# Expert layer: 128 of 512 tokens by gathered weight rows and VectorE sums, 384 by dense products, result with tokens on partitions

## The chip, the core and the metric

One core of a Trainium2 chip runs the whole kernel. Its engines run their own queues and meet only at semaphores: TensorE (PE, with its weight loads PEld), VectorE (DVE), ScalarE (ACT), GpSimd (POOL) and SyncE (SP), which only issues DMAs. The metric is the device time of one execution in microseconds.

## The reference, cut to what matters

Two blocks run one after the other on 512 tokens of width 1024: attention, pooling, convolution and a gated feed-forward, then three attentions, merged, and an expert layer. The change is in that last layer alone.

```
s1, s2 = q[..., 0, :] @ keys1.T, q[..., 1, :] @ keys2.T      # 8 heads, 128 keys each
v1, i1 = top_k(s1, 16);  v2, i2 = top_k(s2, 16)
sv, si = top_k(v1[..., :, None] + v2[..., None, :], 16)       # 16 of 256 pairs
experts = e1 * 128 + e2;  gates = softmax(sv)                 # 8 * 16 = 128 experts a token, of 16384
a   = einsum('cd,ced->ce', h, u[experts])                     # u, v: 16384 x 1024
act = gelu(a) * gates
out = einsum('ce,ced->cd', act, v[experts])
x   = x + out
```

## The kernel before

No row of `u` or `v` is looked up. All 16384 experts are computed for all 512 tokens, and a dense table of gates, zero nearly everywhere, selects. Weights come as slabs of 128 x 2048 (1 MB) in one stream; SyncE loads them into two `raw` buffers, GpSimd splits each into a high and a low part (`W_hi`, `W_lo`), and each exact product is three products (high x high, high x low, low x high), so that TensorE issues three matmuls, each with its weights loaded anew.

The expert layer runs over these stages:

- For each of 8 heads: the query product, scores (TensorE), the two top 16 and the top 16 of pairs (VectorE). One slab of `u` is multiplied beside each head (`u_half`, 2 x 8 x 3 matmuls of 512 tokens a slab), then 8 more slabs while VectorE turns the choices into expert numbers and gates (`picks`). ScalarE applies gelu to each result and stores it in HBM (`gelu_dram`).
- The other 48 slabs of `u`. For each token VectorE makes two one-hot rows (lines 1673 and 1674), and TensorE multiplies them (line 802) into the token's 128 x 128 table of gates; ScalarE collects 64 tokens and stores 4 MB (`gates_dram`). TensorE issues one such product after every three matmuls of `u_half`. 4 of 6 slabs have tokens beside them (16 each).
- 64 slabs of `v`. For each, SyncE loads the gelu values and the gates of its 256 experts (a pair, `gelu_in` and `g_in`), VectorE multiplies them (`gated`, line 1681), ScalarE copies the product to `B_hi` (line 1220), VectorE subtracts for `B_lo` (line 1687), and TensorE adds 48 matmuls into all eight banks, features on partitions (`outputs_of`, lines 817 to 819). At the end VectorE adds the banks to X, and one DMA stores 2 MB.

Every engine's order is the order in which the code is written; nothing is scheduled. GpSimd splits slab s (`split_whole`, lines 379 to 385) when it is loaded (`slab_loaded`) and TensorE has used slab s-2 (`slab_used`). Its `slab_split` releases TensorE and also SyncE's next load into that `raw` buffer. A pair is loaded when the pair two before has been multiplied (`act_ready`).

Of the kernel before, what the change touches and what calls it, by code (L numbers as in the profile page):

```python
# [35 lines left out]
GB = T // GT  # L36


U_PICKS, U_TOKENS, U_BETWEEN = 8, 4, 2
assert HEADS + U_PICKS + GB * (U_TOKENS + U_BETWEEN) == PAIRS and GT % (8 * U_TOKENS) == 0  # L40
U_AT = HEADS + U_PICKS

# [29 lines left out]
ARENA = 19170  # L72
# [14 lines left out]
def build(nc, x_in, stream, cols_in, tables_in, mem_in, keys_in, out):  # L87
    g_dram = nc.dram_tensor("gates_dram", [GB, P, KEYS, GT], F32, kind="Internal").ap()
    gelu_dram = nc.dram_tensor("gelu_dram", [PAIRS, P, 2 * T], F32, kind="Internal").ap()

    with ExitStack() as ctx:
# [21 lines left out]
        tab = sb("tab", [P, 512])  # L113
        col = sb("col", [P, N_COLS])
# [8 lines left out]
        bank = [ctx.enter_context(nc.psum_tensor(f"bank{i}", [P, 512], F32)) for i in range(8)]  # L123
# [54 lines left out]
        top_f = [bank[1 + q // 2][:, 256 * (q % 2):256 * (q % 2) + 256].rearrange("p (h s) -> p h s", h=HEADS)  # L178
# [4 lines left out]
        picks_t = at(16384, 3, T)  # L183
        iota = at(17920, KEYS)
        hot = at(18048, 4, 2, KEYS)
# [4 lines left out]
        gelu_in, g_in, prod = at(0, 2, 2 * T), at(2048, 2, 2 * T), at(4096, 2, 2 * T)  # L190
        gelu_out = B_plain[:, 0:4, :]

# [6 lines left out]
        slab_half = sem("slab_half")  # L199
# [33 lines left out]
        x_done, stored = sem("x_done"), sem("stored")  # L233

# [73 lines left out]
        def _(sp):  # L308
# [40 lines left out]
            def pair(s, j):  # L349
# [7 lines left out]
                sp.dma_start(gelu_in[:, j, :], gelu_dram[s + j, :, :]).then_inc(pair_loaded[j], 16)  # L357
# [12 lines left out]
            sp.wait_ge(x_done, 1)  # L370
            sp.dma_start(out.rearrange("(k p) t -> p k t", p=P), X[:, :, :]).then_inc(stored, 16)
            sp.wait_ge(stored, 16)
# [3 lines left out]
        def _(pool):  # L376
            def split_whole(s, j, ada=N_ADA - 4):

                pool.wait_ge(slab_loaded[j], s * 8 + (8 * ada + 16))
                pool.wait_ge(slab_used, s + (j - 1))  # L380
                pool.tensor_tensor(beat[:, :], zero[:, :], zero[:, :], ALU.add)  # L381
                pool.tensor_copy(W_hi[:, j, :], raw[:, j, :]).then_inc(slab_half, 1)  # L382
                pool.wait_ge(slab_half, s + (IN_PARTS * (PARTS - 1) + j + 1))
                pool.tensor_tensor(W_lo[:, j, :], raw[:, j, :], W_hi[:, j, :].bitcast(F32), ALU.subtract)\  # L384
                    .then_inc(slab_split, 1)
# [42 lines left out]
            if n % 2:  # L428
                split_whole(n - 1, 0)
# [3 lines left out]
        def _(pe):  # L433
# [309 lines left out]
            def u_half(s, odd, j, before=N_MID, token=None):  # L743
# [3 lines left out]
                if not isinstance(s, int) or s + odd > 0:  # L747
                    pe.wait_ge(gelu_ready, s * 2 + (2 * odd + j - 1))
                for k in range(KD):
                    (lh, ll), (rh, rl) = w_tile(slot, D * j + P * k), act_tile("A", k)  # L750
                    mm(bank[6 + j][:, :], lh, rh, start=k == 0, stop=False)  # L751
                    mm(bank[6 + j][:, :], lh, rl, start=False, stop=False)  # L752
                    last = mm(bank[6 + j][:, :], ll, rh, start=False, stop=k == KD - 1)  # L753
# [28 lines left out]
            for q in range(QT):  # L782
# [8 lines left out]
            for q in range(GB):  # L791
                per_half = GT // (2 * U_TOKENS)
                first = U_AT + (U_TOKENS + U_BETWEEN) * q
                with pe.Fori(0, U_TOKENS - 1, 2) as s:
                    t = s * (2 * per_half)
                    for half in range(4):
                        def token(k):
                            j = per_half * half + k
# [7 lines left out]
                u_slabs(first + U_TOKENS, U_BETWEEN)  # L806


            def outputs_of(s, odd, first=False, final=False):
# [3 lines left out]
                for j in range(2):  # L813
                    for m in range(KD):
                        lh, ll = w_tile(slot, D * j + P * m)
                        rh, rl = act_tile("B", 4 + 2 * odd + j)
                        mm(bank[m][:, :], lh, rh, start=first and j == 0, stop=False, skip_group_check=True)  # L817
                        mm(bank[m][:, :], lh, rl, start=False, stop=False, skip_group_check=True)  # L818
                        last = mm(bank[m][:, :], ll, rh, start=False, stop=final and j == 1, skip_group_check=True)  # L819
                last.then_inc(slab_used, 1)  # L820

            pe.wait_ge(g_copied, T + 8)
            pe.wait_ge(gelu_ready, KEYS)
            outputs_of(0, 0, first=True)
            outputs_of(0, 1)
            with pe.Fori(2, PAIRS - 3, 2) as s:
                for odd in range(2):
                    outputs_of(s, odd)
# [5 lines left out]
        def _(act):  # L834
# [310 lines left out]
            def gelus(s, odd=0, tokens=None):  # L1145
# [3 lines left out]
                for j in range(2):  # L1149
# [11 lines left out]
                    act.activation(out_[:, j, :], bank[6 + j][:, :], ACT.Gelu).then_inc(gelu_ready, 1)  # L1161
# [69 lines left out]
        def _(dve):  # L1231
# [459 lines left out]
            for j in range(2):  # L1691
                gated(0, j)
# [139 lines left out]
```

## Time and profile before

| | |
|---|---|
| median of 3 runs | 3113.04 us (3111.86 to 3113.2) |
| the profiled execution | 3113.2 us, its span 3111.4 us |
| busy | PE 94%, POOL 55%, DVE 49%, ACT 21% |
| granted TensorE clock, whole span | 0.967 |
| expert layer, from the first scores | 1458 to 3111 us |

A matmul's recorded duration (0.39 us for 512 columns) holds its latency in the pipeline; its cost in a stream is the distance between two starts. A DMA is recorded at its issue on its queue (SPq, ACTq), and the time to its landing stands in the DMA view. An idle time in brackets in a timeline is that just before the row, with what ended it.

### The profile page before, as it was taken

The page shows a single profiled execution, that of the slowest core. Times are in us where ns is not written, and L with a number is a line of the kernel's source. Part 1 is how long each engine was busy: PE and PEld are TensorE (multiplying, and loading weights), DVE is VectorE, ACT ScalarE, POOL GpSimd, SP SyncE. Part 2 cuts the span into 40 slices and gives each one's busy share as a digit, 9 for nine tenths or more (in the row PEclk, how much of TensorE's full clock was granted, in tenths as well). Part 3 has the DMA queues.
Part 4 walks back from the last instruction along what each step waited for, and adds up shares of the span by engine and source line. Part 5 has one row for each costly group of instructions (what it writes and reads, how often), then busy time and mean ns, then how long its engine had stood idle before and what let it go on. Part 6 is the DMA issues. An engine that isn't in the chain of part 4 may idle for free.

```text
span 3111.4 us, 40021 instructions
## 1 busy us (share of the span) xinstructions
PE 2915.2 (94%) x13606; PEld 2346.7 (75%) x13606; DVE 1528.7 (49%) x2999; ACT 659.0 (21%) x1262; POOL 1703.2 (55%) x1248
## 2 busy tenths in 40 slices
PE   4977799998999899998999999999998999999998
PEld 3855588886866656776877888888887888888886
DVE  4466421113432344544889555555554555555553
ACT  4167110002223243331001111121111010000000
POOL 3745466766511615664555445544454666666664
PEclk8988899999989999999999999999999999999999
DMA  5223222222100212212233344444446455555553
GB/s 229 95 90 138 78 82 95 95 95 99 68 28 28 71 41 70 94 68 89 108 110 122 118 173 176 162 176 169 176 167 218 168 196 196 195 189 189 190 196 127
DMA packets 126527, 402.18 MB, mean 129 GB/s; under 512 B 7504, under 2 KB 74704, under 8 KB 93904
## 3 DMA queue, kind: packets, MB, share of 16 engines
q1 hardware_dynamic: 113280, 328.75, 30.2%
q10 hardware_dynamic: 13136, 71.89, 5.9%
q8 instruction: 77, 1.26, 0.2%
q14 instruction: 34, 0.28, 0.0%
HBM read 331.40 MB, written 69.21 MB: 129 GB/s over the span
## 4 chain that ended last, share of the span: by engine, by line
PE 88%; DVE 5%; ACT 3%; DMA 1%; issue 1%; POOL 1%; ACTq 0%; SPq 0%; DVEq 0%; POOLq 0%
PE bank L487 8%; PE bank L489 8%; PE bank L488 8%; PE bank L817 7%; PE bank L819 7%; PE bank L818 7%; PE bank L751 7%; PE bank L752 7%; PE bank L753 7%; PE bank L802 4%; PE bank L617 2%; PE bank L635 2%; PE bank L593 2%; PE bank L637 1%; PE bank L636 1%; PE bank L521 1%
## 5 line engine op out<-in xcount | busy, mean ns | idle before, releaser
L384 POOL TENSOR_TENSOR W_lo<-raw,W_hi 128x2048 fp32r<-128x2048 f32 x127 | 637.9, 5023 | 10.2
L400 POOL TENSOR_TENSOR W_lo<-raw,W_hi 128x512 fp32r<-128x512 f32 x376 | 494.0, 1324 | 0.0
L751 PE MATMUL bank<-A_hi,W_hi 128*128 128x512 f32 x1024 | 449.2, 439 | 3.9 <-ACT B_plain L1161 2.9
L817 PE MATMUL bank<-B_hi,W_hi 128*128 128x512 f32 x1024 | 399.1, 390 | 10.3 <-DVE B_lo L1687 10.3
L752 PE MATMUL bank<-A_lo,W_hi 128*128 128x512 f32 x1024 | 403.5, 394 | 0.0
L753 PE MATMUL bank<-A_hi,W_lo 128*128 128x512 f32 x1024 | 403.5, 394 | 0.0
L819 PE MATMUL bank<-B_hi,W_lo 128*128 128x512 f32 x1024 | 398.8, 389 | 0.0
L818 PE MATMUL bank<-B_lo,W_hi 128*128 128x512 f32 x1024 | 398.8, 389 | 0.0
L403 POOL TENSOR_TENSOR beat<-zero 128x1 f32<-128x1 f32 x94 | 19.3, 205 | 658.1 <-PE bank L637 255.8
L381 POOL TENSOR_TENSOR beat<-zero 128x1 f32<-128x1 f32 x127 | 24.6, 194 | 638.6 <-PE bank L753 401.8
L1673 DVE TENSOR_SCALAR arena<-bank,arena 128x128 f32<-128x128 f32 x512 | 179.7, 351 | 301.8 <-PE bank L802 282.0
L1681 DVE TENSOR_TENSOR arena<-arena 128x1024 f32<-128x1024 f32 x64 | 232.3, 3630 | 141.5 <-DMA arena<-gates_dram 141.5
L487 PE MATMUL bank<-A_hi,W_hi 128*128 128x512 f32 x680 | 265.8, 391 | 4.9 <-issue 4.9
L489 PE MATMUL bank<-A_hi,W_lo 128*128 128x512 f32 x680 | 264.7, 389 | 0.0
L488 PE MATMUL bank<-A_lo,W_hi 128*128 128x512 f32 x680 | 264.6, 389 | 0.0
L395 POOL CAST W_hi<-raw 128x512 fp32r<-128x512 f32 x376 | 248.6, 676 | 0.0
L382 POOL CAST W_hi<-raw 128x2048 fp32r<-128x2048 f32 x127 | 241.1, 1899 | 0.0
L1687 DVE TENSOR_TENSOR B_lo<-arena,B_hi 128x1024 fp32r<-128x1024 f32 x64 | 132.2, 2066 | 208.4 <-ACT B_hi L1220 208.4
L817 PEld LDWEIGHTS bank<-B_hi,W_hi 128*128 128x128 f32 x1024 | 192.6, 188 | 50.6 <-issue 10.6
L802 PEld LDWEIGHTS bank<-arena 128*128 128x128 f32 x1024 | 193.0, 188 | 46.5
L753 PEld LDWEIGHTS bank<-A_hi,W_lo 128*128 128x128 f32 x1024 | 192.4, 188 | 45.3
L818 PEld LDWEIGHTS bank<-B_lo,W_hi 128*128 128x128 f32 x1024 | 192.6, 188 | 40.0
(234 smaller groups left out, 5207.3 us busy)
## 6 DMA issues: line engine op xcount, KB each, us to landing
raw<-weights SPq DMA_DIRECT2D x241, 1024.0 KB, 4.8
gelu_dram<-B_plain ACTq DMA_DIRECT2D x64, 512.0 KB, 2.6
gates_dram<-arena ACTq DMA_DIRECT2D x8, 4096.0 KB, 14.9
arena<-gelu_dram SPq DMA_DIRECT2D x64, 512.0 KB, 5.6
arena<-gates_dram SPq DMA_DIRECT2D x64, 512.0 KB, 6.9
W_plain<-weights SPq DMA_DIRECT2D x4, 1024.0 KB, 15.9
X<-x_t SPq DMA_DIRECT2D x1, 2048.0 KB, 14.1
out_t<-X SPq DMA_DIRECT2D x1, 2048.0 KB, 7.2
```

The lines of the kernel that those rows point to most:

```text
L384: pool.tensor_tensor(W_lo[:, j, :], raw[:, j, :], W_hi[:, j, :].bitcast(F32), ALU.subtract)\
L400: return pool.tensor_tensor(W_lo[:, j, cols], raw[:, j, cols], W_hi[:, j, cols].bitcast(F32), ALU.subtract)
L487: mm(to, lh, rh, start=i == 0, stop=False)
L488: mm(to, lh, rl, start=False, stop=False)
L489: last = mm(to, ll, rh, start=False, stop=i == n - 1)
L751: mm(bank[6 + j][:, :], lh, rh, start=k == 0, stop=False)
L752: mm(bank[6 + j][:, :], lh, rl, start=False, stop=False)
L753: last = mm(bank[6 + j][:, :], ll, rh, start=False, stop=k == KD - 1)
L802: mm(bank[4 + j // 4 % 2][:, P * (j % 4):P * (j % 4) + P], hot[:, j % 4, 0, :], hot[:, j % 4, 1, :], start=True, stop=True).then_inc(hot_u ...
L817: mm(bank[m][:, :], lh, rh, start=first and j == 0, stop=False, skip_group_check=True)
L818: mm(bank[m][:, :], lh, rl, start=False, stop=False, skip_group_check=True)
L819: last = mm(bank[m][:, :], ll, rh, start=False, stop=final and j == 1, skip_group_check=True)
```

## The change

The last 128 tokens leave the dense path. Their expert numbers (`index`) and gates are computed first among the picks, with tokens on partitions. During the `u` slabs GpSimd issues 128 indirect DMAs, each gathering one row of `u` (4 KB) per token, and VectorE forms the sum over each row times the token's hidden row (`dot`), which TensorE has transposed into PSUM (`h_rows`). During the `v` slabs GpSimd issues 128 more, two a slab, and VectorE adds each gathered row times its activation to `y_rows`, two banks of PSUM (`add_rows`). The dense path works on 384 tokens (`TD`): matmuls of `u_half` have 384 columns, the gate tables are 6 of 64 tokens, five groups of 8 slabs with 8 tokens each, then 4 slabs with 16 and 4 without.

The `v` stage is turned round: activations are the weights (`lhs`), 128 tokens at a time, and the slab is the moving operand, 512 columns, for three token blocks: 36 matmuls a slab. X is first transposed into the banks (32 matmuls), so that nothing is added at the end; each block is copied to SBUF and stored by itself. In this stage ScalarE makes `W_hi` (`high`), and GpSimd makes only `W_lo` (`low_of`).

```diff
-U_PICKS, U_TOKENS, U_BETWEEN = 8, 4, 2
+TD = T - P
+U_BLOCKS = ((8, 0), (8, 0), (8, 0), (8, 0), (8, 0), (4, 4))
+SLOTS = 128
+DOTS, DOT_TOKENS = 8, 20
+V_GATHERS = SLOTS // PAIRS
...
 # GpSimd
-            with pool.Fori(IN_PARTS, n - n % 2 - 1, 2) as s:
-                for j in range(2):
-                    split_whole(s, j)
+            def gather(k, got, rows, gathered, used):
+                if k >= 4:
+                    pool.wait_ge(used, k - 3)
+                pool.indirect_dma_start(got[k % 4], None, rows, bass.IndirectOffsetOnAxis(ap=index[:, k:k + 1].bitcast(U32), axis=0))\
+                    .then_inc(gathered[k % 4], 16)
+            n_u = 0
+            for s in range(IN_PARTS, N_MID + PAIRS + 2):
+                split_whole(s)
+                if s >= HOT_AT and n_u < SLOTS:
+                    if s == HOT_AT:
+                        pool.wait_ge(index_ready, 1)
+                    upto = min(SLOTS, (s - HOT_AT) * 8 * DOTS // DOT_TOKENS + 3)
+                    for k in range(n_u, upto):
+                        gather(k, u_got, u_rows, u_gathered, u_dotted)
+                    n_u = upto
+            for i in range(2):
+                pool.wait_ge(g_stored[i], 8 * GB)
+            for s in range(N_MID + PAIRS + 1, N_MID + 2 * PAIRS + 1):
+                if N_MID + PAIRS + 2 <= s < n:
+                    pool.wait_ge(v_half, s - (N_MID + PAIRS + 1))
+                    low_of(s)
+                k = V_GATHERS * (s - (N_MID + PAIRS + 1))
+                for i in range(V_GATHERS):
+                    gather(k + i, v_got, v_rows, v_gathered, v_added)
...
 # TensorE
-                    mm(bank[6 + j][:, :], lh, rh, start=k == 0, stop=False)
+                    mm(to, lh, rh, start=k == 0, stop=False)          # to = bank[6 + j][:, 0:TD]
...
+            pe.wait_ge(u_dotted, SLOTS)
+            for q in (QT - 1, *range(QT - 1)):
+                for m in range(KD):
+                    last = mm(two_banks[q][:, P * m:P * m + P], X[:, m, P * q:P * q + P], ident, start=m % 4 == 0, stop=False,
+                              skip_group_check=True)
+                last.then_inc(x_rows_ready, 1)
...
+                def part(q, half, j):
+                    to = two_banks[q][:, 512 * half:512 * half + 512]
+                    lh, ll = act_tile("B", 4 + 2 * odd + j, P * q, P)
+                    rh, rl = w_tile(slot, D * j + 512 * half, 512)
+                    mm(to, lh, rh, start=False, stop=False, skip_group_check=True)
+                    mm(to, ll, rh, start=False, stop=False, skip_group_check=True)
+                    return mm(to, lh, rl, start=False, stop=final and j == 1, skip_group_check=True)
...
 # ScalarE
+            def high(s, j):
+                slab = s + (j + N_MID + PAIRS)
+                slot = (N_MID + PAIRS + j) % 2
+                act.wait_ge(slab_loaded[slot], s * 8 + (8 * (N_MID + PAIRS + j - slot + N_ADA - 4) + 16))
+                act.wait_ge(slab_used, slab - 1)
+                act.activation(W_hi[:, slot, :], raw[:, slot, :], ACT.Copy).then_inc(v_half, 1)
...
             with act.Fori(2, PAIRS - 1, 2) as s:
                 for j in range(2):
+                    high(s, j)
                     operand(s, j)
...
 # VectorE
+            def dot(k, c):
+                dve.wait_ge(u_gathered[c % 4], k * 4 + (16 * (c // 4) + 16))
+                dve.scalar_tensor_tensor(out=u_got[c % 4], in0=u_got[c % 4], scalar=1.0, in1=h_rows[:, :], op0=ALU.mult,
+                                         op1=ALU.mult, accum_out=dots[:, bass.ds(k + c, 1)]).then_inc(u_dotted, 1)
+            with dve.Fori(0, SLOTS // DOTS, 1) as n:
+                c = 0
+                for j in range(DOT_TOKENS):
+                    one_hot(n * DOT_TOKENS, j)
+                    if (j + 1) * DOTS // DOT_TOKENS > c:
+                        dot(n * DOTS, c)
+                        c += 1
...
+            def add_rows(s, j):
+                for i in range(V_GATHERS):
+                    k = s * V_GATHERS + (V_GATHERS * j + i)
+                    c = V_GATHERS * j + i
+                    dve.wait_ge(v_gathered[c], s * (8 * V_GATHERS // 2) + 16)
+                    dve.wait_ge(v_added, k)
+                    dve.scalar_tensor_tensor(out=y_rows[:, :], in0=v_got[c], scalar=dots[:, bass.ds(k, 1)], in1=y_rows[:, :],
+                                             op0=ALU.mult, op1=ALU.add).then_inc(v_added, 1)
...
             for j in range(2):
                 gated(0, j)
+            dve.wait_ge(x_rows_ready, 1)
+            for j in range(2):
+                add_rows(0, j)
             with dve.Fori(2, PAIRS - 1, 2) as s:
                 for j in range(2):
                     gated(s, j)
+                    add_rows(s, j)
```

GpSimd's queue in the `v` stage, before: the body of the loop over slabs, one slab of each parity (`beat` is a dummy; the cast makes `W_hi`).

```order
L380 REGISTER_ALU [waits slab_loaded0]
L381 TENSOR_TENSOR beat<-zero 128x1 [waits slab_used]
L382 CAST W_hi<-raw 128x2048
L383 REGISTER_ALU
L384 TENSOR_TENSOR W_lo<-raw,W_hi 128x2048 [waits slab_half]
```

The same queue afterwards, from the last whole split (slab 1 of `v`) on. The two DMA rows after it are gathers 0 and 1, which serve pair 0; the first `W_lo` row that waits for `v_half` is slab 2, and the two gathers behind it serve pair 1.

```order
L411 CAST W_hi<-raw 128x2048 [waits slab_used,slab_loaded0]
L403 TENSOR_TENSOR W_lo<-raw,W_hi 128x2048 [waits slab_half]
L458 DMA arena<-v_rows,arena 128x1024 [waits g_stored1,g_stored0]
L458 DMA arena<-v_rows,arena 128x1024
L403 TENSOR_TENSOR W_lo<-raw,W_hi 128x2048 [waits v_half]
```

The cast is gone from the loop, and every `W_lo` is followed by two gathers that stand behind it, for the pair one before.

ScalarE's queue in the loop over `v` slabs, before (two slabs) and then afterwards (one slab and the start of the next):

```order
L1219 REGISTER_ALU [waits act_ready]
L1220 ACTIVATE B_hi<-arena 128x1024 [waits slab_used]
L1217 REGISTER_ALU
L1219 REGISTER_ALU [waits act_ready]
L1220 ACTIVATE B_hi<-arena 128x1024 [waits slab_used]
```

```order
L1302 REGISTER_ALU [waits slab_loaded1]
L1303 ACTIVATE W_hi<-raw 128x2048 [waits slab_used]
L1307 REGISTER_ALU
L1310 ACTIVATE B_hi<-arena 128x2x384 [waits slab_used,act_ready]
L1301 REGISTER_ALU
L1302 REGISTER_ALU [waits slab_loaded0]
L1303 ACTIVATE W_hi<-raw 128x2048 [waits slab_used]
```

`W_hi` of the next slab now stands behind `B_hi` of this one.

VectorE's queue afterwards in the same loop, one slab; before, it had only the first two operations (`arena` here is the product `prod`, `banks` is `y_rows`):

```order
L1802 TENSOR_TENSOR arena<-arena 128x768 [waits pair_loaded0]
L1807 REGISTER_ALU
L1808 TENSOR_TENSOR B_lo<-arena,B_hi 128x2x384 [waits act_hi_ready]
L1817 ISA
L1818 REGISTER_ALU [waits v_gathered0]
L1819 ISA [waits v_added]
L1819 SCALAR_TENSOR_TENSOR banks<-arena,banks 128x1024
```

The two additions of a slab now stand between its `B_lo` and the gating of the next slab, each behind a wait for its gathered rows.

## Rows read from the trace of the kernel before

**Rows 1.** The page, its first line.

```profile
span 3111.4 us, 40021 instructions
```

**Rows 2.** Windows by stage: busy us of each engine, PEclk, DMA share, GB/s.

```profile
1458.00:1650.00 192.00, 186.86 (x870) 154.21 (x871) 168.04 (x806) 20.19 (x32) 108.04 (x87) 0.99 0.29 105
1650.00:1738.00 88.00, 84.29 (x364) 68.97 (x362) 69.79 (x64) 11.39 (x18) 49.22 (x24) 0.98 0.37 138
...
1742.00:2390.00 648.00, 648.00 (x3326) 546.87 (x3325) 341.87 (x1023) 126.44 (x223) 313.31 (x142) 1.00 0.45 167
2390.00:2402.00 12.00, 1.75 (x6) 1.13 (x5) 7.44 (x3) 1.74 (x3) 6.52 (x3) 0.65 0.94 327
2402.00:3098.00 696.00, 696.00 (x3069) 576.17 (x3068) 356.98 (x125) 66.87 (x63) 464.60 (x186) 1.00 0.54 184
```

**Rows 3.** TensorE's timeline (start, duration): 256-column products, then 512-column ones.

```profile
145.18 0.28 PE L487 MATMUL bank<-W_hi,A_hi 128*128 128x256 f32 x1
...
145.54 0.28 PE L487 MATMUL bank<-W_hi,A_hi 128*128 128x256 f32 x1
...
1699.82 0.39 PE L752 MATMUL bank<-A_lo,W_hi 128*128 128x512 f32 x1
1700.05 0.39 PE L753 MATMUL bank<-A_hi,W_lo 128*128 128x512 f32 x1
```

**Rows 4.** One-hot products (page, part 5), and waits from 1458 to 1742.

```profile
L802 PE MATMUL bank<-arena 128*128 128x128 f32 x1024 | 196.3, 273 | 0.0
...
DVE arena L1603 <- PE bank L773: 22.6, 8, 8.1
...
DVE arena L1673 <- PEq L790: 19.7, 1, 19.7
```

**Rows 5.** GpSimd's timeline in the one-hot stretch, one slab.

```profile
2298.94 1.90 POOL L382 CAST W_hi<-raw 128x2048 fp32r<-128x2048 f32 x1
2300.91 4.60 POOL L384 TENSOR_TENSOR W_lo<-raw,W_hi 128x2048 fp32r<-128x2048 f32 x1
```

**Rows 6.** Timelines of VectorE, GpSimd, ScalarE and SyncE's queue, one slab of values.

```profile
2708.29 2.06 DVE L1687 TENSOR_TENSOR B_lo<-arena,B_hi 128x1024 fp32r<-128x1024 f32 x1 [3.21 <-ACT B_hi L1220]
2712.24 3.65 DVE L1681 TENSOR_TENSOR arena<-arena 128x1024 f32<-128x1024 f32 x1 [1.89 <-DMA arena<-gates_dram]
...
2707.24 0.19 POOL L381 TENSOR_TENSOR beat<-zero 128x1 f32<-128x1 f32 x1 [3.24 <-PE bank L819]
...
2709.35 5.46 POOL L384 TENSOR_TENSOR W_lo<-raw,W_hi 128x2048 fp32r<-128x2048 f32 x1
...
2707.19 1.06 ACT L1220 ACTIVATE B_hi<-arena 128x1024 fp32r<-128x1024 f32 x1 [9.82 <-PE bank L819]
...
2704.18 0.33 SPq L347 DMA_DIRECT2D raw<-weights  x1
2704.86 0.33 SPq L357 DMA_DIRECT2D arena<-gelu_dram  x1
2705.39 0.38 SPq L358 DMA_DIRECT2D arena<-gates_dram  x1
```

**Rows 7.** Groups by line and form: busy us, mean ns of one.

```profile
L1674 DVE TENSOR_SCALAR arena<-bank,arena 128x128 f32<-128x128 f32 x512 | 206.0, 402 | 0.0
...
L1161 ACT ACTIVATE B_plain<-bank 128x512 f32<-128x512 f32 x128 | 76.1, 595 | 318.0 <-PE bank L753 318.0
...
L1220 ACT ACTIVATE B_hi<-arena 128x1024 fp32r<-128x1024 f32 x64 | 68.0, 1063 | 618.9 <-PE bank L819 609.3 <-DVE arena L1681 9.6
...
L1664 DVE TENSOR_TENSOR arena<-arena,bank 128x2048 f32<-128x2048 f32 x8 | 18.3, 2287 | 0.3
...
L1291 DVE SCALAR_TENSOR_TENSOR bank<-X,col,bank 128x512 f32<-128x512 f32 x16 | 11.9, 755 | 0.5
```

**Rows 8.** DMA issues from 1742 to 2390: KB each, median us to landing.

```profile
gelu_dram<-B_plain ACTq DMA_DIRECT2D x47, 512.0 KB, 2.6
```

More of the change, by code:

```diff
@@ L70 @@
     N_TABLE += _width
-ARENA = 19170
+ARENA = 18944
 class Taken:
@@ L781, in _ @@
             stage()
-            for q in range(QT):
+            for k in range(KD):
+                hi, lo = act_tile("A", k, TD, P)
+                to = h_rows[:, P * k:P * k + P]
+                mm(to, hi, ident_r[:, :], start=True, stop=False, skip_group_check=True)
+                last = mm(to, lo, ident_r[:, :], start=False, stop=True, skip_group_check=True)
+            last.then_inc(rows_ready, 1)
+            for q in range(QT - 1):
                 b = turn()
@@ L790, in _ @@
             pe.drain().then_inc(hot_used, 4)
[L791 to L794, printed above, removed]
+            first = U_AT
+            for q, (with_tokens, between) in enumerate(U_BLOCKS):
+                per_half = GT // (2 * with_tokens)
+                every = KD // per_half
+                with pe.Fori(0, with_tokens - 1, 2) as s:
                     t = s * (2 * per_half)
@@ L797, in token @@
                         def token(k):
-                            j = per_half * half + k
+                            if k % every:
+                                return
+                            j = per_half * half + k // every
                             if j % 4 == 0:
@@ L812, in outputs_of @@
                 pe.wait_ge(act_lo_ready, s + (odd + 1))
[L813 to L826, printed above, removed]
+                def part(q, half, j):
[5 more added lines that the diff above has]
+                    return mm(to, lh, rl, start=False, stop=final and j == 1, skip_group_check=True)
+                if final:
+                    for q in range(QT - 1):
+                        for half in range(2):
+                            for j in range(2):
+                                last = part(q, half, j)
+                        last.then_inc(block_done, 1)
+                else:
+                    for j in range(2):
+                        for q in range(QT - 1):
+                            for half in range(2):
+                                last = part(q, half, j)
+                    last.then_inc(slab_used, 1)
+            with pe.Fori(0, PAIRS - 3, 2) as s:
                 for odd in range(2):
@@ L1179, in _ @@
             stage_end()
-            for q in range(QT):
+            for q in range(QT - 1):
                 n = at_["turn"]
@@ L1188, in _ @@
             act.drain().then_inc(g_copied, 8)
-            for q in range(GB):
+            first = U_AT
+            for q, (with_tokens, between) in enumerate(U_BLOCKS):
                 if q >= 2:
```

151 lines of the change are left out of this document (99 added, 52 removed).

## The prediction

> **What bounds the kernel now.** I read the windows by stage first, then TensorE's own timeline for its pace, then who waits for whom at the two edits, then the DMA issues. The span is 3111.4 us [rows 1]. From 1458 us on the expert part has four stretches [rows 2]: scores and picks (192 + 88 us), the stretch with one-hot products (648 us), a 12 us gap, and the value products (696 us). In the 648 and the 696 us TensorE is busy all the time at full clock; everything else waits for it. A 512-column product starts every 0.227 us and a 256-column one every 0.120 us (three in 0.36) [rows 3]; a straight line between them gives 0.1733 us for 384 columns, an estimate. 48 x 0.227 = 10.9 us is one slab before.
>
> **TensorE's part of the change.** First products: 64 slabs x 48, each 0.0534 us shorter: 2.56 us a slab, 8.32 us left. Values: 36 products of 512 columns in place of 48, so 36 x 0.227 = 8.16 us a slab. If TensorE stayed the bound this would be 164 + 174 us, and 128 fewer one-hot products: 648 us less 48 x 10.9 leaves 127 us for 512, 0.247 us each (the row has two records for each), 32 us [rows 2, 4].
>
> **Scores and picks.** 16 slabs x 2.56 = 41 us less on TensorE. VectorE now waits 22.6 us for scores in this stretch [rows 4]: it needs 192 - 22.6 = 169 us of it, about 175 for all 32 units, and TensorE afterwards 192 - 20.5 = 171.5: VectorE takes over. At the end of the picks it has 19.7 us in hand now [rows 4]; afterwards both end near 1697 us. The 16 small transposing products add about 1 us and one transposed block fewer gives half of it back. I take -39 (bounds -30 and -41).
>
> **One-hot stretch.** Five blocks of 8 slabs with 8 tokens each (8.32 + 8 x 0.247 = 10.3 us a slab), then 4 slabs with 16 (12.3) and 4 without (8.3): 412 + 49 + 33 = 494 us if TensorE is the bound. Beside it per 10.3 us slab:
> - GpSimd: 1.90 + 4.60 us of split [rows 5] and 3.2 gathers. The trace of before has no indirect DMA. Bounds for the issue of one: 0.33 us, what SyncE's queue takes [rows 6], and the 4.6 us of the longest GpSimd work here. I take 1.2, for an instruction that moves nothing itself lies nearer the queue's row: 6.5 + 3.8 = 10.3. Just even.
> - VectorE: 8 tokens with two one-hots each, 0.40 us for the longer [rows 7], 6.4 at most, and 3.2 dot products. A three-operand instruction with a PSUM operand takes 0.755 us for 512 elements and 2.29 us is a two-operand one of 2048 [rows 7]: 1.27 for 1024. 3.2 x 1.36 with its accumulator = 4.4. Sum 10.8 at most, 10.3 where neighbours overlap. Also even.
> - DMA: 1.05 MB weights, 3.2 x 0.52 MB rows, 0.39 MB gelu, 0.52 MB gates: 3.65 MB in 10.3 us is 354 GB/s, and the densest stretch of before (94% of the DMA engines' time) moved 327 [rows 2]. So 11.2 us a slab from this alone, and the 4.2 MB gate store comes in one piece, behind which weights and rows are late; the dot products stand in VectorE's queue ahead of the one-hots, so a late row stops TensorE.
> With three limits at or above 10.3 I take 12 us: 480 + 82 = 562, that is -86. Bounds: -154 (no one is late) and +150 (a gather of 3 us: 6.5 + 9.6 = 16 us a slab).
>
> **Value stretch: the wait that the change closes to a ring.** Now GpSimd makes both halves and waits 3.2 us for TensorE in each slab [rows 6]; the gating product follows a DMA, nothing else. In the new order, for slab v (pair v is the gelu and gate pair of that slab):
> 1. GpSimd subtracts W_lo(v), then issues the two gathers for pair v-1 (in its queue they stand behind it).
> 2. VectorE adds pair v-1, then gates pair v (behind the adds in its queue).
> 3. ScalarE makes B_hi(v), then W_hi(v+1) (behind it in its queue).
> 4. GpSimd can subtract W_lo(v+1) only from that.
> Each step waits for the one before, once a slab. It is no pipeline: the ring's length is the slab's time, whatever TensorE needs. Step by step:
> - W_lo: recorded 5.46, but it ran from the end of VectorE's B_lo (2710.35) to 2714.81: 4.46 [rows 6]. In the ring VectorE is idle then. 4.5.
> - two gathers from the end of W_lo until the second has landed: x, below.
> - second add 1.3, the first being done before.
> - gating, 768 elements: 1024 took 2715.89 - 2714.81 = 1.08 once the port was free [rows 6]: 0.9.
> - B_hi: 1024 elements take 1.06 and 512 take 0.60 on ScalarE [rows 7]: 0.85 for 768, and 1.95 for the 2048 of W_hi.
> - six hand-overs of about 0.05 (B_hi ends at 2708.25 and B_lo starts at 2708.29 [rows 6]): 0.3, and 0.1 for GpSimd's start.
> Sum 9.9 + x. For x: at the same moment, the end of W_lo, SyncE issues the next 1.05 MB slab, as it does now at 2704.18, with 2 x 0.52 MB behind it; the last of these landed when gating started, 2712.24: 8.0 us for the same bytes [rows 6]. That is the upper end, as the gathers have a queue of their own and go beside the slab; 2.1 MB at 327 GB/s are 6.4 alone. The lower end is 0.33 x 2 + 2.6 = 3.3, one unhindered 512 KB transfer [rows 8]. I take 7.4, near the upper row: 17.3 us a slab against 10.9 before.
> TensorE is idle for half of each slab; in the 12 us gap at 2390, where it hardly ran, its granted clock was 0.65, near the lower of its two levels, 1.2 of 2.4 GHz [rows 2]. Even at half clock a slab is 2 x 8.16 = 16.3 us, which just fits into the ring and costs nothing.
> The stretch: 32 transposes of X (32 x 0.25 = 8; they cover the first gating, which cost the 12 us gap), slab 0 8.2, W_hi and W_lo of slab 2 6.5: 22.7. Then 61 rings to slab 63: 1055. Then its gathers without a slab beside them 4.6, adds to B_lo 4.0, products 8.2, copy and 512 KB store and end about 5: 22. Sum 1100 us from the last first product on; now that is 3111.4 - 2390.6 = 721. Change +379. The old tail of 13.4 us is inside it.
>
> **Sum.** 3111.4 - 39 - 86 + 379 = 3365; the profiled execution took 1.8 us more than its span and agrees with the median of 3113.0 within 0.2: 3367 us.
>
> A page rule on x: the Trainium skill, "DMA: Bandwidth & Descriptors", section "Anatomy of one DMA — SWDGE (gpsimd) path", gives a GpSimd-issued DMA about 2.0 us plus bytes at 436 GB/s. Two gathers in a row would be an estimated 4.4 us by it, the ring 14.3 and the kernel 3184, which is where rival A comes out from rows; no run here shows such a DMA yet, and the rule knows no slab load beside it.
>
> **Rivals.**
> - A, gathers land early: the slab load does not hold them up. Issue 0.33, one transfer of 2.6 and 0.52 MB / 327 GB/s = 1.6 more for the second: x = 4.5, ring 14.4, 61 x 2.9 = 177 less: 3190. For it: own queue, large rows. Against: DMA engines are shared, and x of the same bytes now is 8.0. Chance 0.14.
> - B, faster: the rows are there before W_lo is done, so the ring does not close, and the value stretch goes by TensorE and the port that VectorE and GpSimd share: gating (0.9) waits for W_lo (4.5) as it does now, 8.16 to 8.8 us a slab. 22.7 + 61 x 8.8 + 22 = 581, -140: 2848. It decides in that place: the kernel is faster once the ring is below (721 + 125 - 45) / 61 = 13.1, so x below 3.2, under my lower bound. For it: four row buffers are allotted, and the wait for a free one asks only for the add two pairs back. Against: the order on GpSimd. Chance 0.1.
> - C, dear gathers: 3 us or more each on GpSimd. 16 us a slab in the one-hot stretch (+150 in place of -86), x = 6 + 2.6 = 8.6: +73. 3676. Against it is only that such an instruction has no data to move. Chance 0.1.
> - D, the change doesn't do what it says (fewer columns do not shorten a product, since loading its weights takes as long): the 256-column pace of 0.120 us excludes it [rows 3]. No chance of its own.
>
> **How the numbers follow.** Ring as worked out 0.66: its own range is x from 5.5 to 8.0 (-116 to +37) and the one-hot stretch from 520 to 620 us (-42 to +58): 3209 to 3462. A 0.14, B 0.1, C 0.1. Faster by over 0.2% (about what a measurement of this kernel can tell from no change): B, 0.1. Within it 0.01, from A and B's border. Slower 0.89. Leaving out B below and C above, the range is 3180 to 3480.
>
> **What would show it.** In the profile after: in the value stretch TensorE busy about half, one W_lo every 17 us, VectorE idle before its add of rows until a v gather, GpSimd idle before W_lo until ScalarE's W_hi, ScalarE idle before B_hi until the gating. Products of 384 columns every 0.173 us. Scores and picks 39 us shorter. GpSimd's gathers near 1.2 us each. The forecast is wrong if TensorE is busy above 90% in the value stretch (B), or if GpSimd is (C).

## The result and the profile after

| | before | after |
|---|---|---|
| median | 3112.45 us (3109.02 to 3113.20, 4 runs) | 3427.34 us (3424.07 to 3431.47, 4 runs) |
| profiled execution, its span | 3113.2, 3111.4 us | 3431.5, 3429.7 us |
| busy | PE 94%, POOL 55%, DVE 49% | PE 80%, POOL 51%, DVE 43% |
| granted TensorE clock | 0.967 | 0.892 |

The ratio is 1.1007, 95% interval 1.0993 to 1.1020: slower. Forecast were 3367 us and a range of 3180 to 3480.

The windows of the changed kernel by stage answer to [rows 2] (columns: busy us of each engine with instruction count, PEclk, DMA share, GB/s):

```profile
1458.00:1650.00 192.00, 174.20 (x910) 155.29 (x908) 175.95 (x834) 21.08 (x36) 116.77 (x83) 0.98 0.31 110
...
1717.00:2318.00 601.00, 519.29 (x3071) 511.32 (x3072) 381.50 (x1024) 95.55 (x191) 426.03 (x220) 0.93 0.71 267
2318.00:2328.00 10.00, 8.02 (x68) 7.54 (x67) 7.14 (x4) 1.64 (x3) 8.90 (x4) 1.00 0.65 219
2328.00:3424.00 1096.00, 670.52 (x2300) 523.41 (x2300) 281.20 (x257) 166.60 (x128) 402.92 (x189) 0.80 0.47 165
```

TensorE no longer fills either long stretch: it is busy 519 of 601 us with one-hots and 671 of 1096 us with values. In the value stretch no other engine is near full either. That is the picture of a ring: everyone waits, nobody is the bound.

The waits of the changed kernel, whole span (us in total, times, longest):

```profile
ACT B_hi L1310 <- DVE arena L1802: 921.2, 64, 15.1
DVE banks L1819 <- DMA arena<-v_rows,arena: 744.0, 66, 12.3
POOL W_lo L403 <- ACT W_hi L1303: 648.9, 62, 10.9
...
PE banks L889 <- DVE B_lo L1808: 426.8, 63, 10.2
```

Each occurs about once a slab. Read in a circle: the gating (L1802) stands behind the sum of rows (L1819), which waits for a gather, which stands behind W_lo, which waits for W_hi, which stands behind B_hi, which waits for the gating. Timelines of one slab (start, duration; in brackets the idle time before and what ended it):

```profile
2912.30 4.55 POOL L403 TENSOR_TENSOR W_lo<-raw,W_hi 128x2048 fp32r<-128x2048 f32 x1 [10.46 <-ACT W_hi L1303]
2916.99 0.96 POOL L458 DMA_INDIRECT arena<-v_rows,arena  x1
2918.25 0.94 POOL L458 DMA_INDIRECT arena<-v_rows,arena  x1 [0.30 <-issue]
2929.80 4.54 POOL L403 TENSOR_TENSOR W_lo<-raw,W_hi 128x2048 fp32r<-128x2048 f32 x1 [10.60 <-ACT W_hi L1303]
...
2923.46 2.72 DVE L1819 SCALAR_TENSOR_TENSOR banks<-arena,banks 128x1024 f32<-128x1024 f32 x2 [12.05 <-DMA arena<-v_rows,arena]
2926.09 0.95 DVE L1802 TENSOR_TENSOR arena<-arena 128x768 f32<-128x768 f32 x1
...
2927.07 0.84 ACT L1310 ACTIVATE B_hi<-arena 128x768 fp32r<-128x768 f32 x1 [14.86 <-DVE arena L1802]
2927.82 1.89 ACT L1303 ACTIVATE W_hi<-raw 128x2048 fp32r<-128x2048 f32 x1
...
2917.04 0.33 SPq L369 DMA_DIRECT2D raw<-weights  x1
```

From W_lo to W_lo it is 17.50 us here; over the stretch, (3399.03 - 2338.28) / 61 = 17.39, from the first and last rings' W_lo. [Rows 6] showed none of this: there GpSimd waited for TensorE, and VectorE for gates.

In the one-hot stretch, the wait for gathered `u` rows is new (waits first, then VectorE's and GpSimd's timelines):

```profile
DVE B_lo_plain L1784 <- DMA B_lo_plain<-u_rows,arena: 162.1, 36, 13.5
...
PE banks L864 <- DVE arena L1777: 81.2, 24, 10.4
...
1956.35 0.40 DVE L1777 TENSOR_SCALAR arena<-banks,arena 128x128 f32<-128x128 f32 x1
1963.15 1.22 DVE L1784 SCALAR_TENSOR_TENSOR B_lo_plain<-B_lo_plain,banks 128x1024 f32<-128x1024 f32 x1 [6.39 <-DMA B_lo_plain<-u_rows,arena]
...
1950.26 1.90 POOL L411 CAST W_hi<-raw 128x2048 fp32r<-128x2048 f32 x1 [6.16 <-PE banks L806]
1952.24 4.60 POOL L403 TENSOR_TENSOR W_lo<-raw,W_hi 128x2048 fp32r<-128x2048 f32 x1
1957.00 0.98 POOL L458 DMA_INDIRECT B_lo_plain<-u_rows,arena  x1 [0.15 <-issue]
```

The row that VectorE wants at 1956.7 was asked for at 1957.00, behind 6.5 us of splitting, and GpSimd had idled 6.2 us before that. The one-hots queue behind the missing row, and TensorE behind them.

The gathers of `u` and of `v` rows follow: first their duration on GpSimd (min/median/max in ns), then, from the DMA view of the whole span, their median time from issue to landing in us:

```profile
L458 POOL DMA_INDIRECT B_lo_plain<-u_rows,arena x128: 935/941/1134, 1709.9 to 2229.2; - x128
L458 POOL DMA_INDIRECT arena<-v_rows,arena x128: 934/951/1533, 2325.2 to 3407.5; - x128
...
B_lo_plain<-u_rows,arena POOLq DMA_INDIRECT x128, 6.3
arena<-v_rows,arena POOLq DMA_INDIRECT x128, 6.1
```

### The profile page after: what moved, and what is told of

Read it like the earlier page. It is cut to its first block, busy times and chain, and to the rows that moved or that the text cites. A ratio compares the mean times of both kernels' runs of the same rounds, so it can differ in the third digit from the quotient of the medians.

```text
span 3429.7 us, 37885 instructions
## 1 busy us (share of the span) xinstructions
PE 2736.6 (80%) x12659; PEld 2260.1 (66%) x12659; DVE 1485.4 (43%) x3128; ACT 724.3 (21%) x1296; POOL 1755.8 (51%) x1315
## 4 chain that ended last, share of the span: by engine, by line
PE 46%; DMA 16%; DVE 13%; POOL 12%; ACT 6%; issue 6%; DVEq 1%; ACTq 0%; POOLq 0%; SPq 0%
DMA arena<-v_rows,arena 11%; POOL W_lo L403 11%; PE banks L539 7%; PE banks L541 6%; PE banks L540 6%; DMA B_lo_plain<-u_rows,arena 4%; ACT W_hi L1303 3%; PE banks L804 3%; PE banks L805 3%; PE banks L806 3%; DVE banks L1819 2%; PE banks L669 2%; DVE arena L1802 2%; PE banks L864 2%; PE banks L687 2%
## 5 line engine op out<-in xcount | busy, mean ns | idle before, releaser
L889 PE MATMUL banks<-W_hi,B_hi 128*128 128x512 f32 x768 | 365.4, 476 | 426.8 <-DVE B_lo L1808 426.8
L889 PEld LDWEIGHTS banks<-W_hi,B_hi 128*128 128x128 f32 x768 | 178.4, 232 | 492.6 <-DVE B_lo L1808 439.6
L1819 DVE SCALAR_TENSOR_TENSOR banks<-arena,banks 128x1024 f32<-128x1024 f32 x128 | 165.0, 1289 | 752.8 <-DMA arena<-v_rows,arena 744.0
L804 PE MATMUL banks<-A_hi,W_hi 128*128 128x384 f32 x1024 | 389.4, 380 | 10.8 <-ACT B_plain L1241 9.8
L805 PE MATMUL banks<-A_lo,W_hi 128*128 128x384 f32 x1024 | 352.1, 344 | 0.0
L806 PE MATMUL banks<-A_hi,W_lo 128*128 128x384 f32 x1024 | 351.9, 344 | 0.0
L890 PE MATMUL banks<-W_hi,B_lo 128*128 128x512 f32 x768 | 349.6, 455 | 0.0
L891 PE MATMUL banks<-W_lo,B_hi 128*128 128x512 f32 x768 | 344.9, 449 | 0.0
L539 PE MATMUL banks<-A_hi,W_hi 128*128 128x512 f32 x680 | 265.8, 391 | 4.9 <-issue 4.9
L541 PE MATMUL banks<-A_hi,W_lo 128*128 128x512 f32 x680 | 264.6, 389 | 0.0
L540 PE MATMUL banks<-A_lo,W_hi 128*128 128x512 f32 x680 | 264.6, 389 | 0.0
L804 PEld LDWEIGHTS banks<-A_hi,W_hi 128*128 128x128 f32 x1024 | 201.3, 197 | 11.4 <-issue 11.4
```

The source lines that it names most:

```text
L539: mm(to, lh, rh, start=i == 0, stop=False)
L540: mm(to, lh, rl, start=False, stop=False)
L541: last = mm(to, ll, rh, start=False, stop=i == n - 1)
L804: mm(to, lh, rh, start=k == 0, stop=False)
L805: mm(to, lh, rl, start=False, stop=False)
L806: last = mm(to, ll, rh, start=False, stop=k == KD - 1)
```

## The experiments

Experiments 1 to 6 change one thing each in the changed kernel, 7 to 11 combine orders; all but experiment 4 compute the same thing. "Pace" is the time from the start of the first value product (L889) to that of the last, over 64 slabs. The changed kernel's is 17.1 us by this measure (17.4 in the ring alone), TensorE's own is 36 x 0.227 = 8.2. The kernel before, on the same chips, took 3112 to 3115 us (medians). Where four executions of a form were taken they lie within 2 to 18 us of each other, one outlier aside, so smaller differences between single runs are not read.

**1. GpSimd's gathers ahead of W_lo.** Cuts the ring at GpSimd.

```diff
-                    low_of(s)                                   # after its wait for v_half
                 for i in range(V_GATHERS):
                     gather(k + i, v_got, v_rows, v_gathered, v_added)
+                    low_of(s)                                   # after its wait for v_half
```

> GpSimd issues the two gathers of a pair ahead of W_lo of the next slab instead of behind it; all else as in the changed kernel. Theory (the ring W_lo -> gathers -> adds -> gating -> B_hi -> W_hi -> W_lo sets the slab's time): the ring is open, TensorE's 8.16 us and the port that VectorE and GpSimd share are left, 9.3 us a slab in place of 17.5: 61 x 8.2 = 500 us less, about 2925 us, and VectorE's waits for gathered rows shrink from 744 us to under 100. Rival (the gathers' own time on the DMA engines sets the pace): the slab stays near 17 us and the time within 50 us of 3427.

Measured 2989.8 us (2982.7 to 3000.9, 4 runs): ratio to before 0.9601, interval 0.9571 to 0.9631. Two swapped statements turn 10% slower into 4% faster. Its value stretch and its largest remaining waits:

```profile
2318.00:2986.00 668.00, 571.12 (x2297) 455.72 (x2296) 307.47 (x256) 168.66 (x127) 439.19 (x189) 0.93 0.75 269
```

```profile
ACT B_hi L1310 <- DVE arena L1802: 431.2, 63, 10.4
DVE banks L1819 <- DMA arena<-v_rows,arena: 300.5, 119, 6.1
...
POOL W_lo L403 <- ACT W_hi L1303: 191.2, 46, 7.0
```

The pace is 10.5 us, not TensorE's 8.2, and the time is 65 us more than expected. The chain of work that ended last shows two rings in its place. The shorter is the old one closed over two slabs: the rows asked for behind W_lo(v-1) hold up gating(v), B_hi(v), W_hi(v+1) and W_lo(v+1); one round took 20.9 us (2387.13 to 2408.06). The longer goes through TensorE: the rows hold up the gating, B_hi and B_lo of slab v, these its 36 products, and these free the buffer for W_hi(v+2), behind which stand W_lo(v+2) and the next gathers. Its longest pieces, from the view of that chain (start, us, what):

```profile
2567.23 8.53 DMA arena<-v_rows,arena
...
2577.19 0.96 DVE arena L1802
...
2590.18 1.93 ACT W_hi L1303
...
2598.75 9.18 DMA arena<-v_rows,arena
```

That is 31.5 us for three slabs, so both rings give 10.5 us a slab. From 2580.06 to 2590.18 the 36 products take 10.1 us and not 8.2, since the first start 0.43 us apart, at the lower level of the granted clock. A row, too, takes longer than before: 7.6 us at the median where it was 6.1.

**2. SyncE's slab load behind the pair of stored tiles** (`pair(s, j)` ahead of `value_slab(s, j)`). The ring's order stays; what changes is what runs beside the gathers.

> SyncE issues a slab's load behind the pair's loads instead of ahead of them, so that it starts after the gating of a slab and not together with the gathers; bytes and all else are the same. Theory of the prediction (the slab load beside the gathers holds them up): the first gathered row lands 4 to 4.5 us after the end of W_lo in place of 6.6, the ring falls from 17.5 to about 15.3 and the time by 130 us to about 3300. Rival (a gather takes its 6 us whatever goes beside it): the ring stays at 17.5 within 0.3 and the time within 20 us of 3427.

Measured 3364.6 us, one run. From 2400 to 2800 us the median `v` row lands in 4.8 us, not 6.1, so the slab load beside it does slow it. The ring shrinks on average from 17.39 to (3332.44 - 2335.56) / 61 = 16.34 us, which is half of what was expected, and so is the gain in time (63 of 130 us). VectorE's timeline shows why:

```profile
2818.21 1.29 DVE L1819 SCALAR_TENSOR_TENSOR banks<-arena,banks 128x1024 f32<-128x1024 f32 x1 [10.08 <-DMA arena<-v_rows,arena]
2820.77 1.29 DVE L1819 SCALAR_TENSOR_TENSOR banks<-arena,banks 128x1024 f32<-128x1024 f32 x1 [1.27 <-DMA arena<-v_rows,arena]
```

The first row comes 4.6 us after W_lo's end (2813.57) in place of 6.6, but now the second sum waits 1.27 us for its own row; in the changed kernel that row was there in time.

**3. ScalarE's W_hi ahead of B_hi** (`high(v+1)` before `operand(v)`). Cuts the ring at ScalarE.

> ScalarE makes W_hi of the next slab ahead of B_hi of this one, not behind it; GpSimd's order is unchanged. Theory (ring): W_hi then waits for TensorE's use of the slab two before alone, and the ring closes over two slabs: W_hi 1.9, W_lo 4.6, first row 6.6, two adds 2.6, gating 0.95, B_hi 0.85, B_lo 0.95, 36 products 8.2: 26.7 us for two slabs, 13.3 each, so 61 x 4.2 = 255 us less, about 3175 us. Rival (ScalarE's order is not part of what closes the ring): no change, 3427 us.

Measured 3439.0 us, one run: nothing gained. The timelines of VectorE, GpSimd and ScalarE say why:

```profile
2911.74 4.63 DVE L1812 TENSOR_TENSOR B_lo<-arena,B_hi 128x768 fp32r<-128x768 f32 x1 [2.86 <-ACT B_hi L1310]
...
2911.05 4.50 POOL L403 TENSOR_TENSOR W_lo<-raw,W_hi 128x2048 fp32r<-128x2048 f32 x1 [10.12 <-ACT W_hi L1303]
...
2909.06 1.91 ACT L1303 ACTIVATE W_hi<-raw 128x2048 fp32r<-128x2048 f32 x1 [14.87 <-PE banks L891]
2910.88 0.83 ACT L1310 ACTIVATE B_hi<-arena 128x768 fp32r<-128x768 f32 x1
2926.42 1.91 ACT L1303 ACTIVATE W_hi<-raw 128x2048 fp32r<-128x2048 f32 x1 [14.71 <-PE banks L891]
```

W_hi(v+1) now waits for the slab that frees its buffer (L891), and B_hi(v), behind it, waits too although its product has long been made. That is another ring: W_hi 1.9, B_hi 0.8, B_lo 4.6 because it meets W_lo (0.96 alone), and the slab's products 10, some 17.3 us in all; the pace is 17.35. The products take 10 us in place of 8.2 because the clock granted over them was 0.84 on average (2916.3 to 2926.4): here, where TensorE stands in the ring, the clock costs time. Moving work ahead of a wait is worth nothing if it brings a wait of its own.

**4. All but the first four `u` gathers left out** (the sums then have factor 0 and no row to wait for; VectorE's instructions stay). It asks what the rows cost the one-hot stretch.

> Left out: all but the first four of the 128 gathers of u rows, and the dot products' scale is 0, so that VectorE does the same 128 dot products on the same four rows without waiting. Theory (late rows and crowded DMA engines stretch the one-hot stretch): it falls from 601 us to near TensorE's own 494, at most 510, and the time to about 3330. Rival (VectorE's own work, one-hots plus dot products, is the bound): it stays above 560 us.

Measured 3312.3 us, one run. From the first one-hot product to the last first product it took 2196.7 - 1711.1 = 485.6 us; in the changed kernel 2317.7 - 1718.1 = 599.6. Its window:

```profile
1711.00:2196.00 485.00, 485.00 (x3064) 484.72 (x3063) 389.98 (x1023) 94.97 (x191) 308.26 (x96) 1.00 0.53 195
```

TensorE is full, and VectorE, with all its instructions, is busy 390 of 485 us and not in the way: asking for the rows and moving them costs the 114 us. In the changed kernel TensorE idles 82 of its 601 us here and is busy 34 us longer than in this run, at a granted clock of 0.93 in place of 1.00.

**5. VectorE's sums one slab later** (`gated(v)` ahead of `add_rows(v-1)`, GpSimd in the changed kernel's order). Cuts the ring at VectorE.

> VectorE takes the two row sums of a slab one slab later: the gating of slab v stands ahead of the sums of slab v-1. GpSimd, SyncE and ScalarE keep the changed kernel's order. Theory (the ring W_lo, gathers, sums, gating, B_hi, W_hi is what makes a slab 17.5 us): the sums leave the ring, which keeps W_lo 4.55 + gating, B_hi and W_hi with handovers of about 4.2, so it no longer closes over one slab and TensorE's products, 8.5 to 10.5 us with the blocked port, set the pace; 62 slabs by 10.5 instead of 17.5 give about 2990 us. Rival 1 (the stretch is long because the row traffic fills the DMA queues, whatever the order): no change, 3427. Rival 2 (GpSimd's next gathers wait for the late sums' buffers and give half back): about 3200.

Measured 2958.6 us, one run; pace 9.8 us. Rows still land late (VectorE waits 278 us for them), but B_hi no longer waits for the sums of the same slab. Rival 1 has fallen, since the DMA queues moved 287 GB/s in this stretch and 165 in the changed kernel, and so has rival 2, which would have given 3200 us.

**6. Gathers two slabs early.** GpSimd issues pair v ahead of W_lo(v), the first four at once.

```diff
+                for k in range(0, 4) if s == N_MID + PAIRS + 1 else [V_GATHERS * (s - (N_MID + PAIRS)) + i for i in range(V_GATHERS)]:
+                    if k < SLOTS:
+                        gather(k, v_got, v_rows, v_gathered, v_added)
                 if N_MID + PAIRS + 2 <= s < n:
...
-                k = V_GATHERS * (s - (N_MID + PAIRS + 1))
-                for i in range(V_GATHERS):
-                    gather(k + i, v_got, v_rows, v_gathered, v_added)
```

> GpSimd issues the two gathers of a slab two slabs earlier than in the changed kernel (the pair of slab v ahead of W_lo of v, the first four at once), so that they wait only for buffers; the other engines keep their order. Theory: rows are there before VectorE asks, the wait of VectorE for row transfers falls from 744 us to under 150 us, a slab takes 9.3 to 10 us against 10.4 with gathers one slab earlier, and the whole is about 2930 us. Rival (in the one-slab-earlier form it was TensorE's products and the shared port that set 10.4 already): 2990, no gain over it.

Measured 2898.9 us, one run; pace 8.9 us, TensorE's clock 1.00 in the stretch. From 2321 us to the end VectorE waits 5.9 us for rows. What is left shows in the timelines of VectorE, GpSimd and ScalarE:

```profile
2601.04 4.99 DVE L1802 TENSOR_TENSOR arena<-arena 128x768 f32<-128x768 f32 x1
...
2600.61 4.60 POOL L403 TENSOR_TENSOR W_lo<-raw,W_hi 128x2048 fp32r<-128x2048 f32 x1 [1.30 <-ACT W_hi L1303]
2605.37 1.50 POOL L458 DMA_INDIRECT arena<-v_rows,arena  x1 [0.15 <-issue]
...
2606.06 0.85 ACT L1310 ACTIVATE B_hi<-arena 128x768 fp32r<-128x768 f32 x1 [5.53 <-DVE arena L1802]
```

The gating now falls beside W_lo and lasts 4.99 instead of 0.95 us; it ends when W_lo has ended and its own 0.9 us are over.

**7 and 8. Orders combined**: experiment 6 with the late slab load of 2; and 1 + 2 + 5 together.

> As the run with gathers two slabs earlier, and SyncE issues a pair's stored activations and gates ahead of the next slab of weights. Theory: a row comes some 1.3 us sooner after its issue (4.8 instead of 6.1 us, as the run with the late slab load showed), which no longer matters where the rows come early: 2900 to 2940 us. Rival: the slab load, now issued later, comes late for the split into its first part and costs 1 us a slab: about 3000.

> Three orders together: GpSimd's gathers ahead of W_lo, VectorE's sums one slab later than the gating, SyncE's slab load behind the pair of stored tiles. Theory: the row sums have over a slab of slack and no operand waits for them; the pace is TensorE's 8.2 us and what the shared port adds: 9.3 to 9.8 us a slab, about 2920 us. Rival: the sums, now late, hold the buffers that the next gathers wait for, and these stand ahead of W_lo on GpSimd: over 10.4 us a slab, 2990 or more.

Measured 2902.2 us for the first (three executions from 2898.8 to 2902.7; a fourth of 14235 us stands alone, its cause unknown), ratio 0.9317, interval 0.9298 to 0.9336; and 2900.7 us for the second (2899.4 to 2901.6), ratio 0.9316, interval 0.9301 to 0.9332. Paces 9.0 and 8.9. Three ways of opening the ring wide enough give the same time. In the timelines of experiment 6, W_lo, gating, B_hi and W_hi go once round in 8.4 us (2600.61 to 2609.04), and the next round takes 9.4 because W_hi waits 1.1 us for TensorE's products. Neither rival came true. One rival stands untested: the DMA engines are busy 0.92 of the time at 324 GB/s (2400 to 2800 us), near the densest stretch of before [rows 2]. That they do not set this pace is shown only by the waits, for in that window no engine waits over 5 us in all for a DMA in any of the three forms. But the 2.88 MB of a slab at 327 GB/s are an estimated 8.8 us, so there is little left below 8.9.

**9 to 11. The `u` gathers, on top of experiment 6.** 9: one row further ahead. 10: a slab's gathers between W_hi and W_lo. 11: both.

```diff
-                    upto = min(SLOTS, (s - HOT_AT) * 8 * DOTS // DOT_TOKENS + 3)
+                    upto = min(SLOTS, (s - HOT_AT) * 8 * DOTS // DOT_TOKENS + 4)    # 9
...
                 pool.tensor_copy(W_hi[:, j, :], raw[:, j, :]).then_inc(slab_half, 1)
+                for k in middle:                                                    # 10
+                    gather(k, u_got, u_rows, u_gathered, u_dotted)
```

> The form with the value gathers two slabs early, and in the one-hot stretch GpSimd issues its u gathers one row further ahead (to four ahead of the tokens of the slab instead of three). In the changed kernel that stretch is 601 us where four gathers alone leave 490. Theory (a row asked for only behind W_lo comes late, and the one-hots queued behind its sum keep TensorE waiting): with one row more in hand most of that goes, 30 to 80 us of the 110, total 2820 to 2870 us. Rival (the sixteen DMA queues' own crowding with gates, gelu tiles and slabs stretches it): 2899, no change.

> As the form with the value gathers two slabs early, and the u gathers of a slab stand between W_hi and W_lo, so that each is asked for some 4.6 us sooner and W_lo comes some 3.8 us later. Theory (rows late behind W_lo): the 6.4 us that VectorE waits behind W_lo fall to about 2, total 2830 to 2870 us. Rival 1 (W_lo, later, becomes what TensorE waits for): no gain or a loss, 2900 to 2950. Rival 2 (crowded queues): 2899.

> Both at once: the slab's u gathers between W_hi and W_lo and one more row behind W_lo. Theory: the best of the three, down to the pace that four gathers alone left (490 us for the stretch), 2800 to 2840 us. Rival (the fourth buffer is asked for while its sum still stands behind one-hots, so GpSimd waits and W_lo is late): not below 2860.

| | total us | first one-hot to last first product |
|---|---|---|
| experiment 6 | 2898.9 | 2311.4 - 1715.0 = 596.4 |
| 9 | 2837.1 (one run) | 2250.0 - 1710.2 = 539.8 |
| 10 | 2844.0 (one run) | 2256.9 - 1709.2 = 547.7 |
| 11 | 2833.3 (2830.7 to 2835.7, 4 runs) | 2243.2 - 1711.3 = 531.9 |

The fastest, 11, stands at 0.9095 of before, interval 0.9080 to 0.9111. Its stretch and its wait for rows:

```profile
1711.00:2243.00 532.00, 496.49 (x3068) 492.59 (x3067) 388.68 (x1023) 95.17 (x191) 428.03 (x219) 0.97 0.82 301
```

```profile
DVE B_lo_plain L1790 <- DMA B_lo_plain<-u_rows,arena: 55.2, 16, 12.1
```

So 68 us of the 114 (599.6 against 531.9) were the order on GpSimd, and one row further ahead alone brings most of that; the 4 us between experiments 9 and 11 are too few to read. The other 46 (531.9 against 485.6) stay. In experiment 11 TensorE waits 32.1 us for one-hots, in four places, and is busy 11 us longer than in experiment 4. The four places go with VectorE's four long waits for a row, of 11.28, 12.08, 11.28 and 11.19 us, each of which ends 19 to 21 us after one of the first four 4 MB gate stores was issued. The second of them, in the timelines of ScalarE's queue and VectorE:

```profile
1887.60 0.52 ACTq L1295 DMA_DIRECT2D gates_dram<-arena  x1
...
1908.64 1.22 DVE L1790 SCALAR_TENSOR_TENSOR B_lo_plain<-B_lo_plain,banks 128x1024 f32<-128x1024 f32 x1 [12.08 <-DMA B_lo_plain<-u_rows,arena]
```

That points at the gate stores, but no run took them away. The rival of experiment 11 is there too, without reaching its price: GpSimd waits 50.4 us for a free row buffer in this stretch.

## Why the prediction was right, point by point

The forecast was 3367 us and the measured time 3427; the direction and the mechanism, a ring of 17.3 us a slab, were right. In the profiled executions the 318.3 us split as follows. The first `u` product starts at 1464.3 in place of 1459.2 us: +5.1, forecast 0. It is no effect of the change: in the variants it starts anywhere from 1455.6 us on, and this was the slowest of the four executions.

- **Scores and picks, -39 forecast, -29 measured** (1718.1 - 1464.3 = 253.8 against 283.1). The mechanism held: VectorE is busy 176 of 192 us and waits 8.6 us in all for scores. The term that was too small is its work: two units of top 16 lie 11.35 us apart, from 1493.50 to 1504.85, so 32 take 181.5 us and not 175, which I had scaled from a stretch with waits in it. That is 6.5 of the 10 us; the rest is not traced.

```profile
1493.50 0.09 DVE L1704 MATCH_VALUE_LOAD arena<-arena,banks 128x8 f32 x1
...
1504.85 0.09 DVE L1704 MATCH_VALUE_LOAD arena<-arena,banks 128x8 f32 x1
```

- **384-column products every 0.1733 us**: right. TensorE's timeline:

```profile
1951.06 0.33 PE L806 MATMUL banks<-A_hi,W_lo 128*128 128x384 f32 x1
1951.23 0.33 PE L804 MATMUL banks<-A_hi,W_hi 128*128 128x384 f32 x1
1951.40 0.33 PE L805 MATMUL banks<-A_lo,W_hi 128*128 128x384 f32 x1
1951.58 0.34 PE L806 MATMUL banks<-A_hi,W_lo 128*128 128x384 f32 x1
```

- **One-hot stretch, -86 forecast, -48 measured**, inside the bounds. TensorE alone was put at 494 us; experiment 4 shows 486 (a slip is in it: 648 less 48 x 10.9 leaves 125 us for the one-hot products, not 127, which is worth 1.5 us). The gather's issue, guessed at 1.2 us, costs 1.25 from one to the next (0.95 and a gap of 0.3). The dot product is 1.21 us, where 1.36 was put down with its accumulator; no row showed that 0.09 us, and the runs show no addition. VectorE, called just even at 10.3 to 10.8 us a slab, was not near its limit (experiment 4). What was too small is the allowance for late rows, 562 - 494 = 68 us against 114: I saw the danger (late rows hold the one-hots) but put it down to the gate stores and traffic, and did not place the gathers in GpSimd's order, where they stand 6.5 us behind the moment from which they could go. Experiments 9 to 11 show that this is over half of it. The upper bound, +150 for a gather of 3 us, doesn't follow from its own line either: 16 us in place of 12 over 40 slabs is 160 us more than -86, so +74, and rival C comes to 3600 us and not 3676. The range did not use it.
- **Value stretch, +379 forecast, +391 measured** (3429.7 - 2317.9 = 1111.8 against 1100). The ring is as drawn, step by step, and 17.39 us where 17.3 was forecast. The step x was right: the second gather is issued at 2918.25 and lands a median of 6.1 us later, an estimated 7.5 us after W_lo's end at 2916.85, where I had 7.4. But the ring does not go through that row. The first sum starts 6.6 us after W_lo's end (2923.46), lasts 1.3 us, and by then the second row is there; so both sums stand in the ring, and the gating starts 9.2 us after W_lo's end, not 8.7. This error is nearly cancelled by another: the hand-overs, put at 0.4 us, come to nothing, as recorded times overlap by up to 0.1 us. That the ring came out within 0.1 us is in part luck. W_lo 4.55, gating 0.95, B_hi 0.84, W_hi 1.89 are within 0.1 of the forecast. Start and end took 1111.8 - 1060.8 = 51 where 45 was put down; part of it is the first gating, 5.23 us beside GpSimd's split.
- **TensorE's clock costs nothing in the ring**: right for the changed kernel. At a mean granted clock of 0.80 its products still end inside the ring: TensorE idles 7.6 us before the slab shown. It is not a rule for rings: in those of experiments 1 and 3 TensorE's products are a part, and the lower clock makes them 10 us in place of 8.2. As TensorE's idle time shrinks the granted clock rises: 0.93 in the stretch of experiment 1, 1.00 in that of experiment 6.
- **Rival A and the Trainium skill's rule** ("DMA: Bandwidth & Descriptors", section "Anatomy of one DMA — SWDGE (gpsimd) path", an estimated 4.4 us for both rows): not so here. By the rule one gather would be an estimated 3.2 us. One takes 6.1 us at the median in this stretch, and 4.8 from 2400 to 2800 us with no slab load beside it (experiment 2). The measurement decides; the rule's figure is too low for rows fetched by index in this kernel. The slab load explains 1.3 of the 2.9 us between them, and where the other 1.6 go was not tested.
- **Rival B** did not come about with this order, but its mechanism is real: with rows asked for in time a slab takes 8.9 us (experiment 6) where it said 8.8, and the kernel 2899 us where it said 2848; most of the difference is the one-hot stretch. Its turning point, a ring of 13.1 us, fits all that was measured: rings of 17.4 and 16.3 us are slower than before, 10.5 and below faster. **Rival C** is out: 0.94 us an issue.

## What to carry to other kernels

When a step moves to another engine, write down for one round who waits for whom in queue order, and look for a circle; its length, not the busiest engine, is the time of a round, and it shows in the profile as every engine well below full, with each waiting about once a round. An asynchronous request (a gather, a load) belongs ahead of the long instruction it does not depend on: here the same instructions took 3427 or 2833 us by nothing but order. Opening a circle at one place is worth only what the next circle leaves, so draw that one too before moving work (experiments 1 and 3).

## What the runs showed of the hardware

- An indirect DMA of 128 rows x 4 KB (0.52 MB) holds GpSimd 0.94 us, two start 1.25 us apart, and it lands 4.8 to 7.6 us after its issue (medians of `v` rows in experiments 2 and 1). What runs beside it matters, above all the slab load: without it 4.8, with it 6.1 (changed kernel). It is not the mean traffic alone, for in experiment 5, at 287 GB/s in place of 165, the median is 6.3. In experiments 6 to 11 its issue lengthens to 1.51 us (median of `v` gathers, beside 0.95 in the changed kernel); VectorE is at work just then, but what lengthens it was not tested.
- A VectorE instruction that meets GpSimd's W_lo can wait for nearly the whole of it, and its record holds the wait: B_lo 4.63 us where it takes 0.96 alone, gating 4.99 where it takes 0.95. The sums of rows have one operand in PSUM and take 1.28 to 1.29 us wherever they fall, beside W_lo too (experiment 6). The Trainium skill, "SBUF — State Buffer", section "Who interferes with whom", says that a VectorE instruction with two SBUF inputs contends with a GpSimd instruction that reads SBUF, through a shared read interface, and that one with at most one SBUF input does not, outside VectorE's two-port modes. The trace agrees on both, with the times just given.
- The granted clock of TensorE was 0.50 while a slab's first products ran in the ring (2911.4 to 2917, after 7.6 us without a product) and 0.96 from 2917 to 2921.3. Products of 512 columns start 0.43 us apart at the lower level and 0.227 at the full one. In the changed kernel this costs nothing; in experiments 1 and 3, where the products are part of the ring, it makes them 10 us in place of 8.2.
